# A decoder step on one core: the seven-product scheme of the up projection begins one slot earlier

## The reference, cut to what matters

```python
def conv_ffn(x, buf, p, l):
    u, buf_new = causal_conv(x @ p['ffn_w_up'][l], buf, p['ffn_conv_w'][l])
    u = u + p['ffn_conv_b'][l]
    return (jax.nn.silu(u[..., :D_FF]) * u[..., D_FF:]) @ p['ffn_w_down'][l], buf_new
```

## Time and profile before

| | |
|---|---|
| median of 3 runs | 2850.45 us (2849.91 to 2854.39) |
| profiled execution | 2845.86 us |
| span of its trace | 2844.2 us |
| PE busy | 2716.3 us (96%) |
| DVE busy | 1411.8 us (50%) |
| ACT busy | 1020.4 us (36%) |
| POOL busy | 900.5 us (32%) |
| mean granted PE clock | 0.988 |

### The profile page before, as it was taken

The page is one execution under the profiler, slowest core; times in us unless marked ns, Lnnn a source line. Parts: engine busy times, 40 slices in busy tenths (PEclk is TensorE's granted clock), DMA queues, the critical chain, the costliest instruction groups (busy, mean ns, idle before and its releaser), DMA issues.

```text
span 2844.2 us, 60997 instructions
## 1 busy us (share of the span) xinstructions
PE 2716.3 (96%) x23723; PEld 2248.8 (79%) x23723; DVE 1411.8 (50%) x3233; ACT 1020.4 (36%) x3033; POOL 900.5 (32%) x989
## 2 busy tenths in 40 slices
PE   7999999999999999999999889899998999999998
PEld 4779769997766668998766777669995679868997
DVE  7665546622243316633542565426616875546641
ACT  2233235422432225422655344325512133324531
POOL 0000117773213206774100002118671000115773
PEclk9999999999999999999999999999999999999999
DMA  5420124444233223443433003534442330123442
GB/s 157 157 76 6 39 75 148 135 143 111 81 109 91 76 79 119 134 143 119 130 106 110 6 6 107 168 110 147 135 140 72 119 118 5 25 71 124 134 145 73
DMA packets 356666, 287.97 MB, mean 101 GB/s; under 512 B 74700, under 2 KB 352764, under 8 KB 355996
## 3 DMA queue, kind: packets, MB, share of 16 engines
q1 hardware_dynamic: 337456, 267.03, 30.5%
q10 hardware_dynamic: 14828, 14.93, 1.6%
q0 software_dynamic: 4096, 2.11, 0.4%
HBM read 263.29 MB, written 20.73 MB: 100 GB/s over the span
## 4 chain that ended last, share of the span: by engine, by line
PE 89%; DVE 5%; issue 3%; ACT 2%; POOL 1%; DMA 0%; ACTq 0%; POOLq 0%; DVEq 0%
PE bank L362 85%; PE bank L3177 1%; PE bank L3200 1%; DVE post_scaled L478 0%; DVE x L481 0%; DVE arena L2849 0%; PE bank L1629 0%; POOL arena L1673 0%; DVE small L1444 0%; ACT squares L432 0%; DVE h L460 0%; DVE h L2008 0%; POOL rstd L421 0%; PE bank L1611 0%; PE bank L2310 0%
## 5 line engine op out<-in xcount | busy, mean ns | idle before, releaser
L362 PE MATMUL bank<-arena 128*128 128x160 f32 (+7 forms) x5898 | 762.9, 292 | 12.2 <-DVE arena L2772 5.1
L362 PE MATMUL bank<-arena,weights 128*128 128x160 f32 (+4 forms) x3376 | 707.5, 368 | 8.6 <-DVE arena L1433 6.6
L362 PEld LDWEIGHTS bank<-arena 128*128 128x128 f32 (+2 forms) x5898 | 662.2, 174 | 37.0 <-issue 14.4
L362 PEld LDWEIGHTS bank<-arena,weights 128*128 128x128 f32 (+2 forms) x3376 | 546.0, 188 | 148.2 <-issue 22.5
L362 PE MATMUL bank<-h,weights 128*128 128x320 f32 (+2 forms) x2576 | 567.9, 373 | 8.4 <-ACT h L447 8.4
L362 PEld LDWEIGHTS bank<-h,weights 128*128 128x128 f32 (+1 forms) x2576 | 431.3, 189 | 127.0 <-issue 17.4
L1673 POOL TENSOR_TENSOR arena<-arena,consts 128x256 f32<-128x256 f32 x30 | 22.9, 763 | 824.0 <-DVE arena L1996 578.3
L362 PE MATMUL bank<-h,arena 64*64 64x64 f32 (+3 forms) x3288 | 217.1, 238 | 2.1 <-DVE h L2008 1.7
L569 POOL TENSOR_TENSOR arena<-weights 128x512 f32<-128x512 f32 (+1 forms) x120 | 148.9, 1241 | 158.0 <-DMA weights<-ffn_w_up 70.0
L362 PEld LDWEIGHTS bank<-h,arena 64*64 64x64 f32 (+1 forms) x3288 | 190.9, 147 | 6.6 <-DVE h L2008 2.8
L771 ACT ACTIVATE bank<-arena,params 128x336 f32<-128x336 f32 x176 | 110.5, 634 | 120.2 <-issue 58.4
(11 more groups left out here) (370 smaller groups left out, 3637.1 us busy)
## 6 DMA issues: line engine op xcount, KB each, us to landing
weights<-ffn_w_up SPq DMA_DIRECT2D x88, 1024.0 KB, 5.1
weights<-ffn_w_down SPq DMA_DIRECT2D x32, 1024.0 KB, 5.1
weights<-rw_wrkv SPq DMA_DIRECT2D x24, 1024.0 KB, 5.0
weights<-gdn_w_in SPq DMA_DIRECT2D x24, 1024.0 KB, 5.4
arena<-cache_mla_latent SPq DMA_DIRECT2D x108, 128.0 KB, 2.3
weights<-ffn_w_down SPq DMA_DIRECT2D x16, 768.0 KB, 4.4
weights<-rw_wo SPq DMA_DIRECT2D x8, 1024.0 KB, 5.0
weights<-gdn_wo SPq DMA_DIRECT2D x8, 1024.0 KB, 5.5
```

The lines of the kernel that those rows point to most:

```text
L362: return pe.matmul(out, lhsT, rhs, start=first, stop=last, skip_group_check=True)
```

## The change

Slot 3 of every layer's up projection becomes a fast slot. It is one number:

```diff
-        FASTS = range(4, 22)
+        FASTS = range(3, 22)
```

## The result

The change makes the kernel slower. The median of five runs is 2878.84 us (2877.58 to 2880.48) against 2849.91 (2845.29 to 2854.39) before: ratio 1.0107, 95% interval 1.0096 to 1.0119. The medians lie 28.9 us apart. The forecast was 2890, range 2866 to 2899. The spans of the two profiled executions are 33.0 us apart (2877.2 and 2844.2).

What follows compares the result with a forecast made beforehand. PE was taken to bound the kernel (89% of the chain of waits). A delay of 8.6 us a layer, PE's -1.00 included, plus 1.3 for the clock, over four layers gave +40: 2890 us, range 2866 to 2899.

Steps and rivals of the forecast that it cites:

- One sign named in the prediction: Start of slot 4 in the changed profile: 8.6 to 10 us after where it did.
- PE's own work: Slot 3 on PE: 16 matmuls of 320 columns become 28 of 160, -1.00 us a layer.
- First collision: Slot 3's four POOL sums beside DVE's eight scalings of h: DVE 2.4 us late.
- Second collision: Slot 4's POOL sums beside DVE's four mixes: mixes end at 442.8, not 436.94; convolution chain 5.8 us late.
- Slot 3 needs the chain: Slot 3's later products wait for ACT and DVE: PE stands nearly 8 us; slot 4 begins 8.6 us later a layer.
- The clock: PE's granted clock falls around the pause in slot 3: +1.3 us a layer, bounds 0 and 2.6.
- No other slot waits: From slot 4 on the chain has room again; no further wait was taken into the forecast.
- the delay is carried on: Rival: slots 4 and 5 wait too, or slot 2 for h; +44 to +50, up to 2900 us; chance 10%.
- smaller collisions: Rival: POOL's early sums disturb nothing, +11, 2861 us; or only DVE's scaling of h, +20, 2871 us; chance 15%.
- The clock stays: Rival: clock stays up or falls too briefly to matter; +8.6 a layer, +34, 2885 us; chance 27%.
- not slower: Rival: PE's saving of 1.00 us a layer comes through; 2846 us, within 0.2% of before; chance 3%.

Runs made afterwards that it cites:

- e6: Changed kernel with slot 3's ACT and DVE instructions moved forward and POOL's block sums started only after DVE's last mix: 2840.50 us, ratio 0.9977 to the kernel before.
- e1: Changed kernel with POOL making slot 3's block sums right after the norm's additions, before waiting for rstd: 2859.72 us, ratio 1.0055 to the kernel before.
- e2: Kernel before (slot 3 plain) with four unread POOL additions of 128x512 where the changed kernel has slot 3's sums: 2853.33 us, ratio 1.0022.
- e4: Changed kernel with 10 unread matmuls of 320 columns added on PE just ahead of slot 3's fifth product: 2875.63 us, ratio 1.0105 to the kernel before.
- e5: Changed kernel with slot 3's instructions moved forward on ACT and DVE, POOL's sums left in place: 2859.30 us, ratio 1.0040 to the kernel before.

## Why the prediction was right, and where it was off

The direction, the mechanism and its place held. The time lay in the range, 11 us under the forecast. The errors below all have the same sign, so none made up for another. One sign named in the prediction did not come: slot 4 began 7.4 us later, counted from the block's start, and not 8.6 to 10. By the steps:

- *PE's own work, -1.00 us a layer:* right. e6 shows it alone.
- *First collision, 2.4 us late:* in place and kind right (e1, e2), in size 1.7. The first drain began at 432.93 and not 433.4, and the block itself began 0.14 later. I had charged each of the four sums with its whole spacing of 1.22 us, as if the later of two instructions waited for the whole of the other. The eight scalings took 7.53 us from the first start to the start of the drain, 4.25 more than the 3.28 of their own, so a sum held DVE up by 1.06.
- *Second collision, another 3.4:* this is the term that was off most; it measured 2.1. I let all four mixes stand behind a sum. In the trace the first mix was issued at 434.78 and POOL's first sum at 434.94, so that mix ran at its own 0.72 and only three waited. By these start times, the 0.6 us by which the scalings were done earlier decided who came first; the other order was not run. The mixes ended 3.9 us later relative to the block's start, not 5.8: 1.7 and 2.1 for the two collisions.
- *Slot 3 needs the chain:* right. Without the collisions' delay I had worked out +2.7 a layer as a rival; the measured 6.68 of e4 less 3.86 of delay is 2.8. e5 and e6 show that it is the place of S1C, TT and C22 in ACT's and DVE's order that costs it. The wait was 6.4 us and not 8, in step with the smaller delay.
- *The clock, +1.3 a layer, bounds 0 to 2.6:* right that it falls, 0.48 to 1.18 in size, mean 0.75 (after less e4). In layer 0 it had fallen some three microseconds before the restart, and nearly four of the slow stretch were left for the products, where the earlier trace rows had 5.3.
- *No other slot waits:* right. The only new wait of any size in PE's list is that for S1C, and slot 2 did not wait for h (64 records without a gap from 424.14). The rival "the delay is carried on" is refuted by this. The sixth product started when the slowed fifth was done, at 452.42, with TT there at 451.85 + 0.32 = 452.17, so the wait for TT was swallowed by the slow clock, as the prediction allowed.

So 4 x (8.6 + 1.3) = 39.6 became 4 x 7.42 = 29.7: 1.9 less a layer for the collisions, 0.55 less for the clock.

Of the rivals, "smaller collisions" was nearest in what was wrong, though neither of its cases came true. "The clock stays" is refuted by the 0.50 rows, and "not slower" by the waits. The gain of the seven-product slot is real, as e6 shows; in the changed kernel it was lost in waiting.

## What to carry to other kernels

A slot whose later matmuls need a bank to be read first is not only shorter on PE: it needs ACT and DVE earlier than a plain slot does, and PE waits by as much as those engines are behind. Before such an exchange read, in the order of these two engines, when they can serve the first such slot, and put its small instructions ahead of the long ones. And in a kernel like this one, new work on POOL should not start on the same event as a run of DVE instructions with two SBUF inputs. The four sums of 1.2 us were ready some 9 us before PE wanted them, and four additions of the same size cost 2.19 us a layer even where nobody read them (e2).

## What the runs showed of the hardware that was not expected

A single wait of 2.55 us, with PE busy without a gap before it, was enough for the granted clock to fall (e1, layer 1). The same wait in all four layers of e1 cost very different amounts: an estimated 2.9 us in layer 0 and 0.4 to 0.8 in the others.

The clock's fall depends on more than the length of a pause. In e5_forward layers 0 and 1 run the same instructions with the same two waits, 1.47 and 1.18 us with one product between. Windows of 4 us, layer 0 first:

```profile
446.00:450.00 4.00, 2.82 (x12) 2.59 (x11) 3.40 (x12) 3.94 (x16) 3.92 (x4) 0.57 0.00 0
450.00:454.00 4.00, 4.00 (x19) 4.00 (x19) 3.50 (x9) 2.18 (x8) 1.86 (x2) 0.58 0.16 39
```

```profile
1102.00:1106.00 4.00, 2.82 (x21) 2.58 (x21) 3.42 (x12) 3.91 (x13) 3.92 (x5) 1.00 0.00 0
```

These windows hold the second wait. PE was busy for 2.82 of 4 us both times, yet the clock fell in one and stayed in the other. The windows just before them, 442 to 446 and 1098 to 1102, are alike too, with 2.53 us busy and a clock of 1.00. The fall cost 2.46 us (5.08 against 2.62). That is more than in the changed kernel with its pause of 6.4 us (0.48 to 1.18), where in layer 0 about half of the slow time lay in the pause itself. What decides whether a short wait costs the clock was not tested.

A DVE instruction held up by a POOL sum did not lose the whole 1.22 us of the sum, but 1.06 for a scaling. In the mixes DVE's first instruction was only 0.16 us ahead of POOL's (434.78 and 434.94), and it ran at its own speed while the three after it did not.
